# Seven quarter-block products for twelve column tiles of an output projection, and two reordered waits, in a two-block transformer kernel on one core

## The reference

```python
hl2 = modulate(rms_norm(xl, norm2_g[l]), mod_l[3], mod_l[4])
xl = xl + mod_l[5][:, None, :] * sq_relu_ffn(hl2, w_ff1[l], b_ff1[l], w_ff2[l], b_ff2[l])
...
def ab_layer(h, w_in, gla_w_gate, gla_b_gate, gla_norm_g, w_out):
    ...
    y = jnp.concatenate([ya, yb], axis=-1) * jax.nn.silu(gate)
    return y @ w_out
...
hn = rmsnorm(h, norm_g[l])        # of the cd layer
z = h @ w_in
u, qd, fd, idd, gate = jnp.split(z, CD_SPLIT, axis=-1)
```

## Time and profile before

| what | value |
|---|---|
| median of 3 executions | 3276.44 us (3273.45 to 3278.1) |
| the profiled execution, its own time | 3273.77 us |
| its span, first to last instruction | 3271.8 us |
| TensorE busy | 3189.9 us, 97% |
| VectorE busy | 1467.8 us, 45% |
| mean granted TensorE clock | 0.979 |
| DMA | 547.71 MB, 167 GB/s over the span |

### The profile page before, as it was taken

The page is one execution under the profiler, slowest core; times in us unless marked ns, Lnnn a source line. Parts: engine busy times, 40 slices in busy tenths (PEclk is TensorE's granted clock), DMA queues, the critical chain, the costliest instruction groups (busy, mean ns, idle before and its releaser), DMA issues.

```text
span 3271.8 us, 43199 instructions
## 1 busy us (share of the span) xinstructions
PE 3189.9 (97%) x19060; PEld 2760.5 (84%) x19068; DVE 1467.8 (45%) x2316; ACT 340.1 (10%) x640; POOL 60.3 (2%) x116
## 2 busy tenths in 40 slices
PE   6899999999999999899999999999999999999998
PEld 1588855478888888799999999989988888899887
DVE  1247635321221013466666677763221124996632
ACT  1110000013230000011110000001012101100010
POOL 0000000020000000000000000000000000000000
PEclk7799998999999999999999999999999999999999
DMA  8986745764444555654555555555455555554343
GB/s 341 342 268 206 246 166 208 258 160 119 129 126 145 153 154 147 147 179 155 173 163 168 168 168 168 167 142 136 110 142 141 142 155 139 145 142 116 103 142 116
DMA packets 715971, 547.71 MB, mean 167 GB/s; under 512 B 23909, under 2 KB 697280, under 8 KB 702989
## 3 DMA queue, kind: packets, MB, share of 16 engines
q1 hardware_dynamic: 687616, 467.69, 48.7%
q0 software_dynamic: 10832, 70.41, 5.8%
q10 hardware_dynamic: 17341, 6.90, 0.8%
HBM read 542.75 MB, written 2.22 MB: 167 GB/s over the span
## 4 chain that ended last, share of the span: by engine, by line
PE 93%; DMA 3%; DVE 2%; ACTq 1%; issue 0%; ACT 0%; DVEq 0%; POOLq 0%
PE psum L415 55%; PE psum L702 7%; PE psum L443 5%; PE psum L694 5%; PE psum L741 2%; PE psum L739 2%; PE psum L734 2%; PE psum L729 2%; PE psum L731 2%; PE psum L740 2%; PE psum L726 2%; DMA ring<-w_mod 2%; DMA arena<-w_mod 1%; PE psum L784 1%; PE psum L593 1%; PE psum L455 1%
## 5 line engine op out<-in xcount | busy, mean ns | idle before, releaser
L415 PE MATMUL psum<-arena,ring 128*128 128x256 f32 (+2 forms) x8192 | 1854.9, 387 | 8.0 <-DVE arena L1807 4.0
L415 PEld LDWEIGHTS psum<-arena,ring 128*128 128x128 f32 x8192 | 1554.5, 191 | 287.7 <-issue 84.7
L702 PE MATMUL psum<-arena 128*128 128x128 f32 x1920 | 219.3, 275 | 0.0
L702 PEld LDWEIGHTS psum<-arena 128*128 128x128 f32 x1920 | 216.8, 192 | 0.0
L1584 DVE SCALAR_TENSOR_TENSOR arena<-arena,cvec 128x2048 f32<-128x2048 f32 x60 | 141.1, 2351 | 140.0 <-DMA arena<-w_mod 139.0
L694 PE MATMUL psum<-arena,ring 128*128 128x128 f32 x1440 | 167.7, 277 | 12.7 <-DVE arena L2070 12.7
L694 PEld LDWEIGHTS psum<-arena,ring 128*128 128x128 f32 x1440 | 164.9, 194 | 13.2 <-DVE arena L2070 13.1
L443 PE MATMUL psum<-ring,arena 128*128 128x128 f32 x1536 | 173.2, 275 | 0.0
L443 PEld LDWEIGHTS psum<-ring,arena 128*128 128x128 f32 x1536 | 172.5, 192 | 0.5 <-issue 0.4
L2130 DVE TENSOR_TENSOR arena<-ring 128x1024 f32<-128x1024 f32 x64 | 78.4, 1225 | 90.3 <-PE psum L726 89.4
L2101 DVE TENSOR_TENSOR arena<-ring 128x2048 f32<-128x2048 f32 x30 | 68.8, 2292 | 111.3 <-PE psum L702 109.9
(11 more groups left out here) (295 smaller groups left out, 2565.2 us busy)
## 6 DMA issues: line engine op xcount, KB each, us to landing
ring<-w_ff SPq DMA_DIRECT2D x128, 1024.0 KB, 6.1
ring<-w_in SPq DMA_DIRECT2D x104, 1024.0 KB, 5.9
arena<-w_mod POOLq DMA_DIRECT2D x64, 1024.0 KB, 7.0
ring<-ab_w_in SPq DMA_DIRECT2D x56, 1024.0 KB, 5.6
ring<-cd_w_in SPq DMA_DIRECT2D x48, 1024.0 KB, 5.8
ring<-w_mod SPq DMA_DIRECT2D x32, 1024.0 KB, 7.0
ring<-w_o SPq DMA_DIRECT2D x16, 1024.0 KB, 5.9
ring<-ab_w_out SPq DMA_DIRECT2D x16, 1024.0 KB, 6.0
```

Source lines behind the costliest of these rows:

```text
L415: mm = pe.matmul(psum[:, s, m * N:(m + 1) * N], w[:, k, m * P:(m + 1) * P], x(k)[:, 0:N], start=(j == 0), stop=(j == kt - 1))
L702: mm = pe.matmul(o, tb[:, i, j, :], XS[:, t, j, :], start=(j == 0), stop=(j == HT - 1))
```

## The change

- **`ab_out` in pairs.** Its first four column tiles stay whole. The other twelve become a new entry of the stream, `ab_pairs`, and are done as six pairs, with a table `TA` and three tiles of input sums `SA` (plus the seventh). `pair` takes the input as a function (`halves` reads three quarters straight from `Y`). VectorE makes the input sums (`quarter_sums`) when the last tile of `Y` is gated, builds the tables, combines the products and adds them to the residual (`added`), two tiles for each pair.
- **The first posts of `hidden_taken`** move ahead of the eleven DMA issues in ScalarE's list.
- **`second_squares(13)`** moves behind `second_pair(3, 1)` and the residuals of the last two tiles.
- **The place of L662**: in `qkb` from the middle of the second slot to before the third, in `u` from the middle of the first to before the second.
- **`differences_used`** is now waited for from the second pair on and no longer from the third (the new table is one for all pairs; in the feed-forward the first has its own), and so are the two banks in `pair_sums`.
- `leave` is skipped once after a first pair, through `held`; `hidden_slot` no longer tests for it. The releases are the same.

```diff
-    ("ab_out", "ab_w_out_2", 0, 4, 16, 128),
+    ("ab_out", "ab_w_out_2", 0, 1, 16, 128), ("ab_pairs", "ab_w_out_2", 512, 3, 2, 256),
...
+        TA, SA = at(14336, 4, HT, P), [at(o, HT, P) for o in (22528, 28800, 29824, 30848)]
...
+            def halves(x, sums):
+
+                def of(t, j):
+                    if t < 3:
+                        return x[:, 2 * j + (t > 0), P * (t == 2):P * (t == 2) + P]
+                    return sums[t - 3][:, j, :]
+                return of
...
-                one_slot(name, u if name == "qkb" else tiles_of(u), "dve", q, N, mid=sums if q == late else None, **kw)
+                if q == late > 0:
+                    sums()
+                one_slot(name, u if name == "qkb" else tiles_of(u), "dve", q, N, mid=sums if q == late == 0 else None, **kw)
...
-                stream_unscaled("qkb", U2, q, lambda: mean_squares((SUMSQ, SUM2), 4), late=1)
+                stream_unscaled("qkb", U2, q, lambda: mean_squares((SUMSQ, SUM2), 4), late=2)
...
-            for q in range(16):
-                one_slot("ab_out", tiles_of(Y), "dve", q % 4, before=last_gated if q == 0 else None)
+            for q in range(4):
+                one_slot("ab_out", tiles_of(Y), "dve", q, before=last_gated if q == 0 else None)
+            pe.wait_ge(sem("input_sums"), n["input_sums"].next())
+            for p in range(6):
+                pair(p, halves(Y, SA), TA)
...
-                    stream_unscaled("u", U3, q, lambda: mean_squares((SUMSQ,), 4))
+                    stream_unscaled("u", U3, q, lambda: mean_squares((SUMSQ,), 4), late=1)
...
             act.wait_ge(sem("gate_used"), n["gate_used"].next())
 
+            for s in range(4):
+                act.sem_inc(sem("hidden_taken"), n["hidden_taken"].up())
             load(GLW, dram["ab_w_in_2"][:, GLOW:GLOW + 16].rearrange("(k p) c -> p k c", p=P), "load_glw")
...
-            for s in range(4):
-                act.sem_inc(sem("hidden_taken"), n["hidden_taken"].up())
             for s in range(4):
                 hidden(s, s)
...
+            def quarter_sums(x, o, name):
+
+                h = [[x[:, f::2, P * t:P * t + P] for f in range(2)] for t in range(2)]
+                step(v.tensor_tensor(o[0], h[1][0], h[1][1], ALU.add))
+                step(v.tensor_tensor(o[2], h[0][0], h[1][0], ALU.subtract))
+                done()
+                TT(o[1], o[0], h[0][0], ALU.subtract)
+                v.tensor_tensor(o[3], h[0][1], o[1], ALU.subtract).then_inc(sem(name), n[name].up())
+                v.wait_ge(sem(name), n[name].now())
...
-                if p >= 2:
-                    n["differences_used"].n = p
+                if p >= 1:
+                    n["differences_used"].n = fast[0] + p
                     v.wait_ge(sem("differences_used"), n["differences_used"].now())
...
-            second_squares(13)
             second_pair(3, 1)
             second_residual(14)
             second_residual(15)
+            second_squares(13)
             second_squares(14)
...
+            v.wait_ge(sem("gated"), n["gated"].now())
+            quarter_sums(Y, SA, "input_sums")
             no_squares()
-            for k in range(KT):
-                add_in(k, k % 4)
-                gained(U3[:, k, :], k, col("norm_g_2", KT + k))
+            for k in range(3):
+                added(k, k)
                 square(X[:, k, :])
+            w = pair_differences("ab_pairs", 0, TA)
+            added(3, 3)
+            square(X[:, 3, :])
+            pair_sums(0, w, TA)
+            for p in range(6):
+                if p < 5:
+                    w = pair_differences("ab_pairs", p + 1, TA)
+                    pair_sums(p + 1, w, TA)
+                pairs_added(p)
+                for k in (4 + 2 * p, 5 + 2 * p):
+                    added(k)
+                for k in (4 + 2 * p, 5 + 2 * p):
+                    square(X[:, k, :])
```

More of the change, by code:

```diff
@@ L381, in take @@
                 pe.wait_ge(sem(free(c, b)), n[full(c, b)].now(1))
+            held = [True]
             def leave(ins, s):
-                ins.then_inc(sem(f"slot{(s + 3) % 4}_used"), 1)
+                if held[0]:
+                    ins.then_inc(sem(f"slot{(s + 3) % 4}_used"), 1)
+                held[0] = True
             def slots(name, c, body):
@@ L419, in one_slot, with quarters, pair @@
                 mm.then_inc(sem(full(c, s)), n[full(c, s)].up())
+            def quarters(s, f, m):
+                return ring[:, s, :].rearrange("p (i f m c) -> p i f m c", f=2, m=2, c=P)[:, :, f, m]
+            def pair(p, x, tb, mid=None):
+                a, b, s0 = 2 * (p % 2), 2 * (p % 2) + 1, 2 * (p % 2)
+                for s in (s0, s0 + 1):
+                    slot(s, 2 * P)
+                take(a, "dve")
+                take(b, "dve")
+                for o, f, m, t in ((psum[:, a, 0:P], 0, 0, 0), (psum[:, a, P:2 * P], 1, 0, 1),
+                                   (psum[:, b, 3 * P:4 * P], 1, 1, 6)):
+                    for j in range(HT):
+                        mm = pe.matmul(o, quarters(s0 + j // 4, f, m)[:, j % 4], x(t, j), start=(j == 0),
+                                       stop=(j == HT - 1))
+                        if p == 0 and t == j == 0:
+                            leave(mm, s0)
+                            held[0] = False
+                if mid is not None:
+                    mid()
+                pe.wait_ge(sem("weight_sums"), n["weight_sums"].next())
+                for i, t, o in ((0, 3, psum[:, b, P:2 * P]), (1, 5, psum[:, b, 2 * P:3 * P]),
+                                (2, 4, psum[:, a, 2 * P:3 * P]), (3, 2, psum[:, b, 0:P])):
+                    for j in range(HT):
+                        mm = pe.matmul(o, tb[:, i, j, :], x(t, j), start=(j == 0), stop=(j == HT - 1))
+                        if i == 0 and j < 2:
+                            mm.then_inc(sem(f"slot{s0 + j}_used"), 1)
+                    if i == 1:
+                        mm.then_inc(sem("differences_used"), n["differences_used"].up())
+                    elif i == 2:
+                        mm.then_inc(sem(full("dve", a)), n[full("dve", a)].up())
+                    elif i == 3:
+                        mm.then_inc(sem(full("dve", b)), n[full("dve", b)].up())
+            def halves(x, sums):
[4 more added lines that the diff above has]
+                return of
             def tiles_of(x):
@@ L767, in _ @@
             for p in range(30):
-                pair(p, XS, TB0 if p == 0 else TB)
+                pair(p, lambda t, j: XS[:, t, j, :], TB0 if p == 0 else TB)
                 table_turns(p)
@@ L1497, in _, with step, done, TT @@
                 v.wait_ge(sem(free("dve", b)), n[free("dve", b)].now())
+            def step(ins):
+                ins.then_inc(sem("vector_step"), n["vector_step"].up())
+            def done():
+                v.wait_ge(sem("vector_step"), n["vector_step"].now())
+            def TT(o, a, b, op):
+                step(v.tensor_tensor(o, a, b, op))
+                done()
+            fast = [0]
+            def loaded(at_, count):
+                for q in range(at_, at_ + count):
+                    n[f"load_slot{q % 4}"].n = q // 4 + 1
+                    v.wait_ge(sem(f"load_slot{q % 4}"), n[f"load_slot{q % 4}"].now())
```

135 lines of the change are left out of this document (54 added, 81 removed).

## The result

The changed kernel took **3257.32 us** (median of five, 3249.63 to 3262.64) against 3276.44 (3273.45 to 3278.71): ratio 0.994, 95% interval 0.9921 to 0.9959. It is faster, by 19 us. The forecast was 3252.8 with a range of 3247 to 3259. Its profiled execution took 3252.25 us with a span of 3250.3, against 3273.77 and 3271.8.

The account below looks back on a forecast made before the run. TensorE, busy 97% of the span, was taken as the bound, so gains must shorten its work or waits. Terms -14.7 - 1.7 - 1.7 - 7.8 + 2.3 = -23.6 us took 3276.44 to 3252.8 us, range 3247 to 3259.

Parts of the forecast that it names:

- The start of the feed-forward: Ahead of the first feed-forward pair: 12.7 us of TensorE wait and 2.0 us of lower clock go, -14.7 us.
- Rival B: Start of the feed-forward: a thin cover breaks, first pair waits half as long as before, low clock stays; 3261.2 us, chance 0.07.
- The end of the feed-forward: Ahead of qkb: pause falls from 4.0 to 2.3 us, -1.7; clock stays full behind it, another -1.7 (bounds 0 and 1.7).
- The output projection: Six pairs of 12.51 us replace twelve whole tiles of 6.907 us, -7.8 us; preparation costed at nothing.
- the thinnest: Output projection: first pair's table ends at 2641.4, TensorE wants it at 2642.5; 1.1 us of cover, costed at nothing.
- Rival C: Output projection: quarter products don't get cheaper with width, a pair lasts 24.2 us; 3323 us, chance 0.01.
- The start of u: New TensorE wait for the fifteenth tile from the last pair, +2.3 us, clock behind it taken as unaffected.
- D: Rival: the waits move on to a later stage bound by DMA or VectorE, nothing gained; 3276 us, chance 0.02.
- A: Rival: both 2.3 us pauses, at qkb and u, cost the clock 1.7 us each; 3256.2 us, chance 0.15 in part or whole.

Follow-up runs that it names:

- the posts: The kernel before with one edit: ScalarE's first four posts of hidden_taken ahead of its eleven DMA issues; 3260.66 us, ratio 0.9953.
- fourteen tiles: Changed kernel, but first matmul of ff1, qkb and u waits for 14 tiles, the fifteenth and sixteenth for their own; 3245.45 us, again 3245.61.
- third trace of the changed kernel: The changed kernel run a third time, unedited, on one chip with the second run of fourteen tiles; 3253.18 us, ratio 0.9932 to the kernel before.
- the version: The same kernel as fourteen tiles, measured twice: 3245.45 us (ratio 0.9907) and 3245.61 us (0.9908) to the kernel before.
- cover broken: Changed kernel with the output projection's first table begun only after the fourth whole tile is added and squared; 3262.30 us in one execution.
- added wait away: Changed kernel with the added differences_used and bank waits taken back in the feed-forward alone; 3262.07 us in one execution.
- the pairs alone: Changed kernel with the posts and second_squares(13) put back where they were; 3272.20 us, ratio 0.9983 to the kernel before.

## Why the prediction was right, point by point

**The start of the feed-forward** (-14.7): 12.9 us for the wait and 1.8 for the clock behind it, shown alone by the posts. VectorE follows the tiles as I had laid out; the spare time before the first pair is 1.2 us where I had 1.4. Rival B didn't come.

**The end of the feed-forward** (-1.7 and -1.7): the pause is 2.30 as forecast. The second -1.7 is a size I took at one end: it holds in five of seven executions with a pause of 2.3 us there, and in two the pause was charged 1.7 us after all.

**The output projection** (-7.8): pairs of 12.51 us, shown in the changed kernel's trace. The covers that I counted on hold, and what breaking the thinnest costs (1.4 us, once) is shown. Rival C is out: a 128-column record keeps its 112 ns with these operands. The ratio that I estimated from the Trainium skill's spacings (the page "TensorE: Matmul & The Clock Gate", section Back-to-back issue gap) isn't met by these float32 matmuls: by it a pair would be 1.45 times two whole tiles, and it is 12.51 / 13.81 = 0.91.

**The start of u** (+2.3): a row of 2.24 us that costs 2.5, and fourteen tiles show that it is nothing but the wait for the fifteenth tile. Here too I took the clock at its cheap end; three of eight pauses were charged.

**The rivals.** D didn't come either. A was put as a case with a chance of 0.15, as if the pauses were charged always or never. That step is wrong in kind: with one and the same kernel the charge was 0, 0 and 1.7 us. The row that I leaned on, the pause of 2.0 us behind which the clock was at 1.00, was itself one draw. The same pause of 2.0 us stands in all thirteen traces, and in six of them the clock fell behind it, here in the third trace of the changed kernel, where TensorE was back at work at 1225.55 (columns as above):

```profile
1225.00:1227.00 2.00, 1.45 (x7) 1.30 (x8) 0.52 (x3) 0.00 (x0) 1.26 (x4) 0.99 0.03 8
1227.00:1229.00 2.00, 2.00 (x6) 1.58 (x5) 0.00 (x0) 0.00 (x0) 0.00 (x0) 0.50 0.65 172
1229.00:1231.00 2.00, 2.00 (x7) 1.59 (x6) 0.00 (x0) 0.00 (x0) 0.00 (x0) 0.66 1.13 316
```

One trace can't give the price of a short pause. The charge belongs in the sum as a mean: five of the fifteen pauses of 2.24 to 2.31 us were charged, so 1.7 x 5 / 15 = 0.6 us for each, 1.1 for both, and in the range as 0 to 3.4. With it the forecast would have been a gain of 22.5 us and 3253.9. The three medians of the changed kernel are 3257.32, 3253.54 and 3253.18, each below the kernel before beside it by 19.1, 22.1 and 21.4 us. That the first trace met the sum so closely is in part luck: it happened to be one in which neither pause was charged.

**What stays of the first median.** It lies 4.5 us above the forecast, and charges at the two pauses can make at most 3.4 of that. The other place where the traces differ by so much is the start, which wasn't changed: up to the first ones it took 1341.3 to 1355.4 us in thirteen traces, 14 us apart, while the stretch behind it repeats within 0.4 us in the three traces of the changed kernel and within 0.3 in the two of the version, once the charges are taken off. TensorE waits for loads in the start. The three longest starts (cover broken, fourteen tiles for the second time, added wait away) each hold a wait of 4.6 to 5.3 us for a load of w_in that no other trace has. The waits for w_mod were 24.4 us in all in the trace of the kernel before and 28.4 in that of the changed kernel, whose start was 2.5 us longer. Does the change itself lengthen the start? The medians speak against it. As an estimate, the median less 2.0 us around the span and less the stretch (1928.7 before; 1904.8 and 1.1 for charges after) leaves starts of 1343.9 to 1346.1 us for the four medians of the kernel before, and 1349.4, 1345.6 and 1345.3 for the changed kernel: only the first lies apart. Why those five executions were longer and scattered more than later ones (13, 5.4 and 7.3 us) wasn't tested, and only one of them has a trace.

## What to carry to other kernels

When an engine waits for a post that costs nothing, look at what stands ahead of it in the poster's queue: four increments behind eleven DMA issues cost 14.7 us, more than all the work saved by seven products for eight. A product built of late-arriving parts should wait for each part where it is needed, not for nearly all at the start: two constants took away both pauses that were left, and with them the charges (none at either place in two traces), for 3245.5 us, the fastest version here. And where executions scatter by more than the effect, compare a stretch between two landmarks of the trace that lie behind the scatter.

## What the runs showed that I had not expected

A pause of 2.3 us can bring the clock down after it is over. In the third trace of the changed kernel TensorE starts qkb at 2151.40, and the windows (columns as above) show the fall in the one from 2151 and the rise in that from 2155, as in the pairs alone:

```profile
2149.00:2151.00 2.00, 0.09 (x1) 0.00 (x0) 1.63 (x5) 0.00 (x0) 0.00 (x0) 1.00 0.00 0
2151.00:2153.00 2.00, 1.60 (x5) 1.41 (x6) 1.90 (x6) 0.00 (x0) 0.00 (x0) 0.74 0.03 8
2153.00:2155.00 2.00, 2.00 (x6) 1.55 (x6) 1.86 (x5) 0.00 (x0) 0.00 (x0) 0.50 0.85 232
2155.00:2157.00 2.00, 2.00 (x10) 1.73 (x9) 1.83 (x6) 0.00 (x0) 0.00 (x0) 0.90 1.08 286
```

The charge is all or nothing: 1.7 us in each of the five cases, 0 in the ten others, at pauses that differ by less than 0.1 us. The pause of 4.0 us was charged in all three traces that have it, but 1.6, 1.7 and 2.6 us.

The pauses are the cause, and not only near it. In windows of 2 us from 1330 to 3230 us of all thirteen traces the granted clock was below 0.99 only in or right behind the waits of the first pair, of qkb, of u and of L784. It stayed at 1.00 at qkb and u in both traces of the version without these pauses, and behind the waits of 1.3 us or less in every trace.

Even one and the same pause brings the clock down at different moments. The wait of 4.8 us at L784 stands in all versions. In the kernel before the clock had fallen inside it, in the window from 3056. In the changed kernel it was still at 1.00 in the last whole window of the pause and fell only in the next one, in which TensorE is back from 3038.29 on:

```profile
3036.00:3038.00 2.00, 0.00 (x0) 0.00 (x0) 1.84 (x3) 0.00 (x0) 0.00 (x0) 1.00 0.00 0
3038.00:3040.00 2.00, 1.71 (x10) 1.74 (x11) 0.83 (x2) 0.00 (x0) 0.00 (x0) 0.71 0.00 0
```

The Trainium skill ("TensorE: Matmul & The Clock Gate", What's actually happening) says that the moment at which the hardware decides runs free of the kernel; what these traces show is what that would give.
